# TensorE issues the scores of an attention pair ahead of the turn of the pair in front of it

## The reference, cut to what matters

```python
s = jnp.einsum('bqgrd,bkgd->bgrqk', qi, k_all).astype(jnp.float32) * d ** -0.5   # scores, 512 keys
p = jax.nn.softmax(s, axis=-1).astype(v_all.dtype)
return jnp.einsum('bgrqk,bkgd->bqgrd', p, v_all)
```

## Time and profile before

| | |
|---|---|
| median of 3 runs | 2814.11 us (2812.05 to 2814.51) |
| the profiled execution | 2816.22 us, span 2814.7 us |
| TensorE busy (matmul) | 2516.1 us, 89% of the span |
| VectorE busy | 1036.4 us, 37% |
| ScalarE busy | 491.4 us, 17% |
| chain that ended last | PE 69%, DMA 16%, DVE 8%, ACT 2% |
| scores (L1421), median record | 589 ns, 288 records |
| turn (L1431), median record | 273 ns, 480 records |

### The profile page before, as it was taken

How to read it: one execution, slowest core, us unless ns; L and a number is a source line. 1 busy time by engine, 2 the same in 40 slices (tenths; PEclk the granted TensorE clock), 3 DMA queues, 4 the chain that set the end, 5 groups by cost and what they waited for, 6 DMA issues and landing times.

```text
span 2814.7 us, 45297 instructions
## 1 busy us (share of the span) xinstructions
PE 2516.1 (89%) x18928; PEld 1540.4 (55%) x18929; DVE 1036.4 (37%) x2408; ACT 491.4 (17%) x978; POOL 246.3 (9%) x406
## 2 busy tenths in 40 slices
PE   7999989999889959999999989999999758878774
PEld 3455545454444457777777545567666434444442
DVE  1226536266464322222222340536456422111112
ACT  2023222222221101111111021323222101110110
POOL 3000000000000011111111100000000021111111
PEclk9999989999999959999999988999999879999998
DMA  9181112133325429999999842123455749999994
GB/s 286 60 358 60 45 47 64 47 131 99 94 96 146 167 100 372 373 372 379 384 374 388 294 129 90 60 94 98 157 176 147 259 193 409 412 414 413 412 400 162
DMA packets 153682, 616.64 MB, mean 219 GB/s; under 512 B 17649, under 2 KB 22065, under 8 KB 137009
## 3 DMA queue, kind: packets, MB, share of 16 engines
q1 hardware_dynamic: 126850, 557.88, 53.0%
q0 software_dynamic: 21584, 36.48, 4.7%
q10 hardware_dynamic: 5152, 20.97, 1.8%
HBM read 598.30 MB, written 46.32 MB: 229 GB/s over the span
## 4 chain that ended last, share of the span: by engine, by line
PE 69%; DMA 16%; DVE 8%; issue 5%; ACT 2%; POOL 1%; SPq 0%; DVEq 0%; POOLq 0%; ACTq 0%
DMA ring<-in_e_down_dram 14%; PE bank L1624 12%; PE bank L1372 12%; PE bank L1266 11%; PE bank L1256 6%; PE score_banks L1641 4%; PE score_banks L1661 3%; PE bank L1385 2%; PE score_banks L1646 2%; PE bank L1543 2%; PE score_banks L1421 2%; PE turned_banks L1431 2%; PE bank L1295 2%; PE bank L1607 1%; PE bank L1445 1%
## 5 line engine op out<-in xcount | busy, mean ns | idle before, releaser
L1624 PEld LDWEIGHTS bank<-scr,ring 128*64 128x64 f32 x8192 | 341.6, 138 | 14.4 <-issue 14.2
L1624 PE MATMUL bank<-scr,ring 128*64 128x96 f32 x8192 | 347.8, 247 | 1.2 <-DVE scr L2329 1.2
L1372 PE MATMUL bank<-HT,ring 128*128 128x512 f32 (+1 forms) x1024 | 343.9, 491 | 0.8 <-ACT scr L987 0.4
L1266 PE MATMUL bank<-ring,HT 128*128 128x512 f32 (+1 forms) x800 | 303.5, 536 | 0.0
L1617 PE MATMUL bank<-ring,scr 128*64 128x256 f32 x2048 | 239.0, 387 | 44.2 <-DMA ring<-in_e_up_dram 21.3
L1372 PEld LDWEIGHTS bank<-HT,ring 128*128 128x128 f32 x1024 | 190.7, 190 | 139.2 <-issue 126.9
L1266 PEld LDWEIGHTS bank<-ring,HT 128*128 128x128 f32 x800 | 151.9, 193 | 142.6 <-issue 136.5
L1617 PEld LDWEIGHTS bank<-ring,scr 128*64 128x64 f32 x2048 | 145.5, 139 | 141.0 <-DMA ring<-in_e_gate_dram 39.3
L1256 PE MATMUL bank<-HT,ring 128*128 128x512 f32 (+1 forms) x512 | 195.0, 539 | 1.8 <-ACT HT L987 1.8
L1661 PE MATMUL score_banks<-ring,scr 128*64 128x512 f32 x512 | 133.5, 669 | 41.6 <-DMA ring<-in_e_down_dram 39.9
L1256 PEld LDWEIGHTS bank<-HT,ring 128*128 128x128 f32 x512 | 96.2, 190 | 91.7 <-issue 88.5
(11 more groups left out here) (261 smaller groups left out, 2759.3 us busy)
## 6 DMA issues: line engine op xcount, KB each, us to landing
ring<-in_e_up_dram SPq DMA_DIRECT2D x64, 2048.0 KB
ring<-in_e_down_dram SPq DMA_DIRECT2D x64, 2048.0 KB
ring<-in_e_gate_dram SPq DMA_DIRECT2D x64, 2048.0 KB
ring<-in_w_in_dram SPq DMA_DIRECT2D x34, 2048.0 KB
ring<-in_w_mod_dram SPq DMA_DIRECT2D x32, 1024.0 KB, 5.3
ring<-in_w_mod_dram SPq DMA_DIRECT2D x8, 2048.0 KB
ys<-consts ACTq DMA_DIRECT2D x1, 12288.0 KB, 39.7
ys<-consts ACTq DMA_DIRECT2D x1, 8192.0 KB, 64.2
```

Source lines behind the costliest of these rows:

```text
L1266: m = pe.matmul(bank[:, 0:width], HT[:, k, t * P:t * P + P], w[:, k, 0:width], start=k == 0, stop=k == KT_D - 1)
L1372: m = pe.matmul(bank[:, 0:NQ], w[:, k, (ft % 4) * P:(ft % 4) * P + P], HT[:, k, 0:NQ], start=k == 0, stop=k == KT_D - 1)
L1624: m = pe.matmul(ps[bank][rows_, f * cap:f * cap + cap], w[:, k, f * P + hf * HALF:f * P + hf * HALF + HALF], XTv[:, k, :], start=k == 0, s ...
```

## The change

The scores of pair i are issued in front of the turn of pair i - 1, instead of behind it. What each of them waits for and sets is unchanged, and so are all other engines' streams.

```diff
                     for i in range(n + 1):
+                        if i < n:
+                            scores(i)
                         if i:
                             turn(i - 1)
-                        if i < n:
-                            scores(i)
                         if i == n and b in "DB":
                             operands_transposed("B" if b == "D" else "C")
```

## The result

The changed kernel takes 2788.28 us (median of 4 runs, 2785.86 to 2794.68), the kernel before, run beside it, 2813.08 us: a ratio of 0.9913, 95% interval 0.9896 to 0.9929, 24.8 us less. The forecast was 17.2 us less, 2797, in a range of 2790 to 2806. The profiled execution took 2787.54 us, 28.7 less than that of before.

What follows compares the result with a forecast made beforehand. In the attention stages the VectorE, ScalarE, VectorE chain sets the pace where TensorE waits for P; elsewhere TensorE runs without a gap. Stage gains 4.3 + 1.7 + 4.9 + 2.7 + 0.6 + 3.0 = 17.2 us give 2797, range 2790 to 2806.

Steps and rivals of the forecast that it cites:

- D's first pair: Start of attention stage D, layer 0: scores run before the turn, the waiting transposes go at 388.05, 2.2 us earlier.
- C's second pair: Stage C, both layers: VectorE gets its scores earlier and no longer waits for them, 1.96 us gained.
- B of layer 1: Stage B, layer 1: gain at 2031 lost to a late bank, the wait of 0.64 stays a gain; 0.6 us.
- C of layer 1: Stage C, layer 1: 1.96 at the start, later 1.06 of scores hidden in a wait; 3.0 us.
- D of layer 1: Stage D, layer 1: peaks start 1.03 earlier, slow scores of 1.67 go into the wait; 2.7 us, between 1.8 and 3.6.
- The waits of L1431: Sign: the turn's waits for normalised P (L2160) in the attention stages fall from 53.8 to about 35 to 40 us.
- the worst reading of the Trainium skill's rule: Turn's first weight load, with its wait, is taken ahead of the scores' matmuls; hiding lost, 9.9 us left of 17.2.
- the clock's return: Rival 1, attention stages: fewer clock falls after waits, 2 to 4.5 us more gain, 2792.5 to 2795 us; chance 0.12.
- Surplus of D: Beyond the forecast for stage D, layer 0: 4.3 us, from earlier VectorE work and scores hidden in waits.
- Surplus of C: Beyond the forecast for stage C, layer 0: 4.9 us, turn 2.95 earlier plus scores of 1.95 to 2.02 hidden.
- Rival 4: Attention stages: splitting waits brings new clock falls, 2.8 us each; nine more make it slower, 2822 us; chance 0.03.
- The hidden scores: Effect (a), scores run inside the turn's wait for P: 1.1, 0.8, 2.0 (D, B, C, layer 0), 1.7, 0.6, 1.1 (layer 1).

Runs made afterwards that it cites:

- the profiled kernel with four steps changed in D: Changed kernel, with the values behind the second fill in steps 2, 12, 14, 16 of D, layer 0: 2786.69 us, ratio 0.9906.

## Why the forecast was right in direction and too small

**What held.** D's first pair went as worked out, step by step (2.4 us against 2.2). The wait of 1.96 us of VectorE at C's second pair is gone, and with the first pair of each stage in the old order these terms came back at 2.6, 2.06 and 2.05 us (forecast 2.2, 1.96, 1.96). In B of layer 1 the gain of one step is lost again to the bank that VectorE frees late, as forecast: that wait grew from 0.76 to 1.72 us. C of layer 1 had gained 3.02 (3.0) by its last values, and a longer wait for the weights of `w_out` (6.60 for 6.34) left 2.76. D of layer 1 gained 2.66 (2.7), but that is partly luck: only 2.01 of it is there behind the wait, where the fill still ran slow (3.09 us), and 0.65 came in the two steps behind. The waits of L1431 went to the scores, by name to L1421; the sum of both, 42.8 us, is a little over the 35 to 40 that I gave. The turn's first weight load was not taken ahead of the scores: at 380.92 the scores run while P is not there yet, so the worst reading of the Trainium skill's rule (TensorE: Matmul & The Clock Gate, Part 2) is not borne out by the trace, and a total of 9.9 us did not come.

**The step that failed** is a sentence in the first part: "Everywhere else there TensorE runs without a gap [...]; there a swap of two TensorE steps changes nothing." (The first half is not quite so either: the earlier trace rows show TensorE waiting 2.13 us at 390.24.) Nothing waits for VectorE there, but the order of two steps decides how many changes of tile shape are in the sequence, and each costs about 0.2 us. The 0.39 us for two changes was measured by itself, and the swap gives 1.9 us in the last 13 steps of layer 0's stages, where I had none. Step by step, between the kernel before and the changed one, a step with no wait and the values directly ahead is 0.19 to 0.20 us shorter. Where a full-tile fill stands directly ahead, both orders have the same number of changes and the gain is 0.04 to 0.06. Together this is 1.2 us in D of layer 0, 1.1 in B and 1.0 in C behind its last wait, 3.3 in all; it is most of the surplus of B (3.00 against 1.7). In layer 1 nearly every step has a fill ahead, so there it gives little; the surplus of B there, 0.5, is such steps and 0.26 in the step whose wait of 0.64 went.

**A second step that failed** is that I gave the clock's return 12% as a rival of its own and nothing in the sum. In D of layer 0 it gave 1.6 us (8.74 to 7.11), at a place I had gone through row by row: I had shortened the idle time of 2.13 to nothing and left the 8.74 us behind it as it was. In C it gave about 0.75: behind the last wait the scores took 2.02 us, of which I had counted the hiding, and the fill 7.89, which I had left as it was; in the changed kernel they take 1.13 and 7.03. The row of the kernel before:

```profile
815.82 7.89 PE L1372 MATMUL bank<-HT,ring 128*128 128x512 f32 x16
```

Of the 0.86 us 0.1 belongs to the shape of the scores that no longer stand ahead of the fill. Surplus of D: 1.6 + 1.2 = 2.8 of 3.2. Surplus of C: 1.0 + 0.75 = 1.75 of 2.1, and another 0.2 is the shape in the step of the last wait. Over the three stages of layer 0 the surplus of 6.6 us is then 3.3 of shape in steps without a wait, 2.4 of clock and 0.9 of small differences at the waits. So the rival was right in part: 2.4 lies in its 2 to 4.5 us, at fewer places than the five it named. Rival 4 put a full fall of the clock at 2.8 us, and the last pair of views of the experiments shows it, 2.82. What it had wrong is that every fall costs that.

**Where a fall of the clock costs something.** Behind the wait of 2.50 us at 763 us of C the profiled kernel with four steps changed in D also had slow scores (2.08) and a slow turn (1.65), and at its next pair it was level with the changed kernel again, as VectorE sets the pace. Only at the stage's last wait, from which on TensorE is the bound to the stage's end, did it cost 2.8.

**The hidden scores.** My 7.3 us for them stand against 12.2 us that are lost when scores wait for P. In D of layer 1 and in B and C of layer 1 the two agree to 0.3 us. In D of layer 0 they do so with the help of a clock that held in one kernel and not in the other, and in B and C of layer 0 that experiment also delays the turn. So the 1.1, 0.8 and 2.0 of layer 0 are neither confirmed nor refuted.

**What stays open.** Why the clock falls behind one wait of 2.33 or 2.50 us and holds behind another of the same length, with the same work around both. In D it goes with the order (behind the wait of 2.33 it fell in the changed kernel, in its repetition and in the one with the first pair put back and held in both with four values moved); in C it differs between kernels with the same order in C. One profile of each kernel can't tell more. Nor is it shown what moves the parts outside the attention stages by some us.

## What to carry to other kernels

Where TensorE is busy throughout, its order can still be worth something: lay float32 matmuls with the same tile shape side by side, and count the changes between 64-row or 64-column tiles and full ones in a repeated step, at about 0.2 us each as measured here. When a forecast removes an idle time of TensorE of 2 us or more, look at the duration of the work behind it too: if its rows are slow, the price of the wait includes them, if nothing else sets the pace there. And an early issue is only as good as its own wait: ahead of the last covering fill it gave everything back here.

## What the runs showed of the hardware

- A change of tile shape between neighbouring float32 matmuls costs about 0.2 us on TensorE at full clock: 0.39 for the two between 128 by 128 and 64 by 128, an estimated 0.34 for the two between 128 by 128 and 128 by 64 (from a step 0.19 shorter and one 0.15 longer), and 0.19 less in the step that saves one (8.28 to 8.09). Between two full tiles the next weight load starts during the matmul in front (571.65 for a matmul at 571.76). The Trainium skill (TensorE: Matmul & The Clock Gate, Part 3, The mechanism) says in one sentence that a weight load overlaps matmuls in flight only when its row group differs, and in another that a load into the background weight buffer is pulled ahead as well. The trace does not agree with the first taken alone: the overlap is there between full tiles, which use the same rows, and is missing from 64 rows to 128. What the load does where the shape changes neither sentence says.
- After idle times of 2.13 and 2.25 us at the start of D the fill took 8.74 and 8.47 instead of 7.11; after 2.33 and 2.50 us the work was slow in some kernels and at full speed in others, and after 3.01 us it was once at full speed. The length of the wait alone doesn't decide it.
